# Reading 40 blocks of expert rows densely instead of gathering them, in the last stage of a decoder layer

## What is computed

```
q = (h @ w_query).reshape(B, S, PEER_HEADS, 2, PEER_HALF)          # 8 heads, 2 halves of 128
s = jnp.einsum('bshcd,hckd->bshck', q, sub_keys)                   # 128 keys for each half
top_s, top_i = lax.top_k(s, PEER_TOPK)                             # 16 of 128
cand = top_s[..., 0, :, None] + top_s[..., 1, None, :]             # 16 x 16 sums
best_s, best_i = lax.top_k(cand, PEER_TOPK)                        # best 16
i1 = ...; i2 = ...; eid = i1 * N_KEYS + i2                         # first key, second key
g = jax.nn.softmax(best_s, axis=-1)
a = jax.nn.gelu(jnp.einsum('td,thkd->thk', hx, expert_u[e]))
peer = jnp.einsum('thk,thkd->td', g * a, expert_v[e])
x = _layernorm(ALPHA * h + peer, ln2_g, ln2_b)
```

## Time and profile before

| | us or share |
|---|---|
| median of three runs | 1778.93 |
| the profiled execution | 1780.05, of which the span of its instructions is 1778.3 |
| DMA during the expert stage, 700 to 1700 us | all 16 engines busy, 427 GB/s |
| TensorE, VectorE, ScalarE, GpSimd busy over the span | 83%, 61%, 23%, 42% |
| U gathers, V gathers | 256 and 256, 1 MB each |

### The profile page before, as it was taken

How to read it: one execution, slowest core, us unless ns; L and a number is a source line. 1 busy time by engine, 2 the same in 40 slices (tenths; PEclk the granted TensorE clock), 3 DMA queues, 4 the chain that set the end, 5 groups by cost and what they waited for, 6 DMA issues and landing times.

```text
span 1778.3 us, 15565 instructions
## 1 busy us (share of the span) xinstructions
PE 1481.4 (83%) x5762; PEld 868.2 (49%) x5762; DVE 1078.2 (61%) x1734; ACT 401.6 (23%) x885; POOL 743.7 (42%) x590
## 2 busy tenths in 40 slices
PE   8999999999979747887887788778787788787875
PEld 7988999988668512333333333333333333233321
DVE  6666646666879996555454645454746454544555
ACT  5665464564101220101101011011010201010200
POOL 3210000000456677455555555555555555455341
PEclk9999999999989868999999999999999999999999
DMA  9876444474999999999999999999999999999996
GB/s 314 284 257 206 119 143 143 143 238 165 372 379 421 389 428 426 428 427 427 428 427 428 427 427 427 427 426 428 427 428 426 427 427 427 428 427 427 427 425 254
DMA packets 154045, 644.61 MB, mean 362 GB/s; under 512 B 11621, under 2 KB 64961, under 8 KB 87921
## 3 DMA queue, kind: packets, MB, share of 16 engines
q0 software_dynamic: 79232, 556.58, 74.9%
q1 hardware_dynamic: 74736, 87.04, 14.7%
HBM read 641.47 MB, written 2.10 MB: 362 GB/s over the span
## 4 chain that ended last, share of the span: by engine, by line
DMA 53%; PE 30%; DVE 9%; POOL 4%; issue 2%; DVEq 1%; ACT 1%; SPq 0%; POOLq 0%; ACTq 0%
DMA v_slot<-in_expert_v_dram,eid 52%; PE psum_all L553 13%; PE psum_all L902 6%; DVE u_slot L1647 5%; PE psum_all L693 4%; POOL u_slot L499 3%; PE psum_all L718 1%; POOL v_slot L514 1%; PE psum_all L674 1%; PE psum_all L578 1%; PE psum_all L580 1%; DMA wq_ring<-in_w_query_dram 0%; PE psum_all L640 0%; DMA xh<-in_x_dram 0%; PE psum_all L681 0%
## 5 line engine op out<-in xcount | busy, mean ns | idle before, releaser
L902 PE MATMUL psum_all<-v_slot,diag 128*128 128x512 f32 x1920 | 889.9, 608 | 249.7 <-DMA v_slot<-in_expert_v_dram,eid 249.7
L1647 DVE SCALAR_TENSOR_TENSOR u_slot<-u_slot,xh 128x2048 f32<-128x2048 f32 x256 | 580.8, 2289 | 467.5 <-DMA u_slot<-in_expert_u_dram,eid 467.2
L902 PEld LDWEIGHTS psum_all<-v_slot,diag 128*128 128x128 f32 x1920 | 349.9, 191 | 789.4 <-issue 397.4
L514 POOL DMA_INDIRECT v_slot<-in_expert_v_dram,eid x256 | 344.3, 1345 | 450.1 <-PE psum_all L902 423.1
L499 POOL DMA_INDIRECT u_slot<-in_expert_u_dram,eid x256 | 362.5, 1416 | 231.2 <-DVE eid L1587 95.8
L1201 ACT ACTIVATE diag<-ident,gate 128x128 f32<-128x128 f32 x256 | 76.4, 387 | 698.6 <-PE psum_all L902 454.9
L1253 DVE TENSOR_TENSOR w_lo<-w_ring,w_hi 128x512 fp32r<-128x512 f32 x240 | 156.4, 687 | 77.7 <-ACT w_hi L930 74.6
L553 PE MATMUL psum_all<-act_hi,w_hi 128*128 128x256 f32 x640 | 185.3, 290 | 1.3 <-DVE w_lo L1253 1.2
L553 PE MATMUL psum_all<-act_lo,w_hi 128*128 128x256 f32 x640 | 181.0, 283 | 0.0
L553 PE MATMUL psum_all<-act_hi,w_lo 128*128 128x256 f32 x640 | 180.5, 282 | 0.0
L930 ACT ACTIVATE w_hi<-w_ring 128x512 fp32r<-128x512 f32 x240 | 139.4, 622 | 42.3 <-PE psum_all L553 42.3
(11 more groups left out here) (263 smaller groups left out, 1033.7 us busy)
## 6 DMA issues: line engine op xcount, KB each, us to landing
w_ring<-in_w_in_dram SPq DMA_DIRECT2D x88, 512.0 KB, 5.0
wo_ring<-in_w_out_dram SPq DMA_DIRECT2D x32, 512.0 KB, 5.2
wq_ring<-in_w_query_dram SPq DMA_DIRECT2D x32, 512.0 KB, 9.8
w_ring<-in_cmp_k_w_dram POOLq DMA_DIRECT2D x16, 512.0 KB, 5.4
w_ring<-in_cmp_v_w_dram POOLq DMA_DIRECT2D x16, 512.0 KB, 4.6
u_slot<-in_expert_u_dram,eid POOLq DMA_INDIRECT x256, 32.3
v_slot<-in_expert_v_dram,eid POOLq DMA_INDIRECT x256, 32.7
xh<-in_x_dram SPq DMA_DIRECT2D x4, 512.0 KB, 7.2
```

The lines of the kernel that those rows point to most:

```text
L514: nc.gpsimd.indirect_dma_start(out=v_slot[m % RV][:, :], out_offset=None, in_=expert_v[0], in_offset=bass.IndirectOffsetOnAxis(ap=eid[:, n ...
L902: ins = nc.tensor.matmul(bank[(4 if n < PH else 0) + q][:, :], diag[:, n % 2, k, :], v_slot[m % RV][:, 512 * q:512 * q + 512], start=first ...
L1647: V.scalar_tensor_tensor(u_slot[m % RU][:, :], u_slot[m % RU][:, :], 1.0, xh[:, n // PH, :], ALU.mult, ALU.mult, accum_out=u_dot[:, n, k:k ...
```

## The change

Expert ids with a first key of 88 to 127 (FD = 40 first keys) are treated apart in the V half.

- The V gathers of units 0 to 14 get `bounds_check=ROWS - 1` with ROWS = 88 x 128, so an index beyond it fetches nothing and leaves the buffer's row as it was. `gates_of` makes the coefficient of such a pick zero in `gate` and keeps the full coefficient in `b_val`. Unit 15 is gathered in full.
- For each tile, TensorE transposes first keys, second keys and coefficients (`pick_transposes`). VectorE builds one-hot matrices for 8 tokens at a time (`hot_rows`, 16 times a tile), TensorE multiplies them (`dense_rows`: eight small matmuls), and ScalarE copies the result out (`dense_out`): a matrix of coefficients for every first key, 128 second keys by 128 tokens.
- SyncE reads the 40 blocks of 128 V rows once, 1 MB each, into the U buffers as the last dots free them (`s_d`). TensorE multiplies each block by the coefficient matrices of both tiles (`dense_mm`), eight matmuls of 512 columns a block.
- The V rows of tile 1 (picks 128 to 255) are no longer TensorE's: VectorE adds all 2048 columns (`add_row`), after the last dot and the one-hot matrices. The layer norm of tile 0 stands between the last ten of these adds.
- V buffers: 7 instead of 8. U and V gathers alternate in a ratio of 11 to 8 up to V pick 128, before which all U gathers go out. The ids of units 10 to 15 are made earlier. The rows ln2_g and ln2_b are loaded when TensorE has used V pick 127.

```diff
-RV = 8
+RV = 7
 AHEAD = 4
-BEHIND = 2
 EARLY_V = 4
-SPLIT = TOPK * (NU - 2)
-HALF = D // 2
 PH = 8
+HALF_U = TOPK * PH
+FD = 40
+FA = 24
+ROWS = (NKEY - FD) * NKEY
+LEAD = 3
+G_TOK = 8
+NG_T = P // G_TOK
+PICKS = (P, P - TOPK)
+IDS_AT = {(0, 4): 1, (8, 9): 10, (9, 1): 11, (9, 9): 12, (10, 1): 13, (10, 9): 14, (11, 1): 15}
+IDS_AT.update({(n, 1): n + 1 for n in range(1, 9)})
+HOT0_AT = {12 * TOPK + 11 * b // 4: b for b in range(NG_T)}
+HOT1_AT = 15 * TOPK + 5
...
-        sp.wait_ge(S["ids_ok"], NU + 1)
+        sp.wait_ge(S["v_used"], HALF_U)
...
+        for f in range(FD):
+            if f < RU:
+                sp.wait_ge(S["dots_done"], TOPK * NU - RU + f + 1)
+            else:
+                sp.wait_ge(S["dense_used"], f - RU + 1)
+            first = ROWS + NKEY * f
+            sp.dma_start(u_slot[f % RU][:, :], expert_v[0][first:first + NKEY, :]).then_inc(s_d[f % RU], 16)
...
-            if m >= RV:
+            if RV <= m < HALF_U + RV:
                 pool.wait_ge(S["v_used"], m - RV + 1)
-                if m - RV >= SPLIT:
-                    pool.wait_ge(S["v_dve"], m - RV - SPLIT + 1)
-            nc.gpsimd.indirect_dma_start(out=v_slot[m % RV][:, :], out_offset=None, in_=expert_v[0],
-                                         in_offset=bass.IndirectOffsetOnAxis(ap=eid[:, n, k:k + 1], axis=0)
-                                         ).then_inc(s_v[m % RV], 16)
+            if m >= HALF_U + RV:
+                pool.wait_ge(S["v_dve"], m - RV - HALF_U + 1)
+            src = bass.IndirectOffsetOnAxis(ap=eid[:, n, k:k + 1], axis=0)
+            if n < NU - 1:
+                nc.gpsimd.indirect_dma_start(out=v_slot[m % RV][:, :], out_offset=None, in_=expert_v[0], in_offset=src,
+                                             bounds_check=ROWS - 1, oob_is_err=False).then_inc(s_v[m % RV], 16)
...
-            while sent < min(TOPK * NU, TOPK * AHEAD + (m + 1) * (NU - AHEAD) // (NU - BEHIND)):
+            while sent < min(TOPK * NU, TOPK * AHEAD + (m + 1) * 11 // 8):
                 gather_u(sent // TOPK, sent % TOPK)
                 sent += 1
+            if m == HALF_U:
+                while sent < TOPK * NU:
+                    gather_u(sent // TOPK, sent % TOPK)
+                    sent += 1
...
+        def pick_transposes(t):
+            pe.wait_ge(S["coef_ok"], (PH, NU - 1)[t])
+            n = PICKS[t]
+            units = slice(PH * t, PH * t + n // TOPK)
+            for i, src in enumerate((b_id[:, 0, units, :], b_id[:, 1, units, :], b_val[:, units, :])):
+                ins = nc.tensor.transpose(bank[2 + t][0:n, P * i:P * i + P], src.rearrange("p n k -> p (n k)"), ident[:, :])
+            ins.then_inc(S["pick_mm"], 1)
+
+        def dense_rows(t, b):
+            g, n = NG_T * t + b, PICKS[t]
+            pe.wait_ge(S["hot_ok"], g + 1)
+            if g >= 2:
+                pe.wait_ge(S["dense_ok"], g - 1)
+            for i in range(G_TOK):
+                ins = nc.tensor.matmul(bank[g % 2][:, FD * i:FD * i + FD], hot2[0:n, g % 2, i, :], hot1[0:n, g % 2, i, :],
+                                       start=True, stop=True, skip_group_check=True)
+            ins.then_inc(S["dense_mm"], 1)
+
+        def dense_mm(t, f):
+            src = dense0[:, f, :] if t == 0 else dense1[f >= FA][:, f - FA * (f >= FA), :]
+            for q in range(4):
+                ins = nc.tensor.matmul(bank[(4 if t == 0 else 0) + q][:, :], src, u_slot[f % RU][:, 512 * q:512 * q + 512],
+                                       start=(t == 1 and f == 0), stop=(f == FD - 1))
+                if f == FD - 1:
+                    ins.then_inc(S[("t0_sum", "t1_sum")[t]], 1)
+            if t and f < FD - RU:
+                ins.then_inc(S["dense_used"], 1)
+
+        for m in range(HALF_U):
+            n, k = divmod(m, TOPK)
+            if k == 0:
+                pe.wait_ge(S["diag_ok"], n + 1)
+            if m == 80:
+                pick_transposes(0)
+            if m >= 94 and m % 2 == 0 and m < 94 + 2 * NG_T:
+                dense_rows(0, (m - 94) // 2)
+            pe.wait_ge(s_v[m % RV], 16 * (m // RV + 1))
+            for q in range(4):
+                ins = nc.tensor.matmul(bank[4 + q][:, :], diag[:, n % 2, k, :], v_slot[m % RV][:, 512 * q:512 * q + 512],
+                                       start=(m == 0), stop=False)
+            ins.then_inc(S["v_used"], 1)
+        for q in range(4):
+            nc.tensor.matmul(bank[4 + q][:, :], ident_a[:, :], xh[:, 0, 512 * q:512 * q + 512], start=False, stop=False)
+        pick_transposes(1)
+        for b in range(NG_T):
+            dense_rows(1, b)
+        for f in range(FD + LEAD):
+            if f < FD:
+                pe.wait_ge(s_d[f % RU], 16 * (f // RU + 1))
+                dense_mm(0, f)
+            if f == LEAD:
+                pe.wait_ge(S["dense_ok"], 2 * NG_T)
+            if f >= LEAD:
+                dense_mm(1, f - LEAD)
...
+        def dense_out(t, b):
+            g = NG_T * t + b
+            act.wait_ge(S["dense_mm"], g + 1)
+            cols = slice(G_TOK * b, G_TOK * b + G_TOK)
+            src = bview(g % 2, G_TOK, FD)
+            if t == 0:
+                nc.scalar.activation(dense0[:, :, cols].rearrange("p f t -> p t f"), src, ACT.Copy
+                                     ).then_inc(S["dense_ok"], 1)
...
+        unit(14)
+        picks_out(1)
+        for b in range(NG_T):
+            if b == 11:
+                unit(15)
+            dense_out(1, b)
+        for t in range(2):
+            root(t)
...
-            V.scalar_tensor_tensor(gate[:, n, :], u_act[:, n, :], g_inv[:, n:n + 1], g_exp[:, n, :],
-                                   ALU.mult, ALU.mult).then_inc(S["coef_ok"], 1)
+            V.scalar_tensor_tensor(b_val[:, n, :], u_dot[:, n, :], g_inv[:, n:n + 1], b_val[:, n, :], ALU.mult, ALU.mult)
+            dve.drain()
+            V.scalar_tensor_tensor(gate[:, n, :], b_id[:, 0, n, :], float(NKEY - FD) if n < NU - 1 else float(NKEY),
+                                   b_val[:, n, :], ALU.is_lt, ALU.mult).then_inc(S["coef_ok"], 1)
...
+        def hot_rows(t, b):
+            g, n = NG_T * t + b, PICKS[t]
+            cols = slice(G_TOK * b, G_TOK * b + G_TOK)
+            if b == 0:
+                dve.wait_ge(S["pick_ok"], t + 1)
+            if g >= 2:
+                dve.wait_ge(S["dense_mm"], g - 1)
+            row, key, coef = (pickT[0:n, t, i, cols].unsqueeze(2) for i in range(3))
+            V.tensor_tensor(hot1[0:n, g % 2, :, :], iota_row[0:n, :].unsqueeze(1).to_broadcast([n, G_TOK, FD]),
+                            row.to_broadcast([n, G_TOK, FD]), ALU.is_equal)
+            V.tensor_tensor(hot2[0:n, g % 2, :, :], iota_key[0:n, :].unsqueeze(1).to_broadcast([n, G_TOK, NKEY]),
+                            key.to_broadcast([n, G_TOK, NKEY]), ALU.is_equal)
+            dve.drain()
+            V.tensor_tensor(hot1[0:n, g % 2, :, :], hot1[0:n, g % 2, :, :], coef.to_broadcast([n, G_TOK, FD]), ALU.mult
+                            ).then_inc(S["hot_ok"], 1)
...
--            V.scalar_tensor_tensor(xh[:, 1, HALF:D], v_slot[m % RV][:, HALF:D], gate[:, n, k:k + 1], xh[:, 1, HALF:D],
-                                   ALU.mult, ALU.add)
+            V.scalar_tensor_tensor(xh[:, 1, :], v_slot[m % RV][:, :], gate[:, n, k:k + 1], xh[:, 1, :], ALU.mult, ALU.add)
             dve.drain().then_inc(S["v_dve"], 1)
...
+                if n and k == (10 if n < NU - 1 else 3):
                     gates_of(n - 1)
+                m = TOPK * n + k
+                if m in HOT0_AT:
+                    hot_rows(0, HOT0_AT[m])
+                if m >= HOT1_AT:
+                    hot_rows(1, m - HOT1_AT)
         gates_of(NU - 1)
...
+        for b in range(TOPK * NU - HOT1_AT, NG_T):
+            hot_rows(1, b)
+        V.tensor_scalar(xh[:, 1, :], xh[:, 1, :], ALPHA, None, ALU.mult)
+        dve.drain()
+        for m in range(HALF_U, TOPK * NU):
+            if m == TOPK * NU - 10:
+                for q in range(4):
+                    dve.wait_ge(S["t0_sum"], q + 1)
+                    V.bn_stats(l2st[:, 0, q, :], bank[4 + q][:, :])
+                stats_of(0)
+            if m == TOPK * NU - 8:
+                dve.wait_ge(S["s_ln2row"], 32)
+                norm_out(0, lambda q: bank[4 + q][:, :], y0)
+            if m == TOPK * NU - 3:
+                for q in range(4):
+                    dve.wait_ge(S["t1_sum"], q + 1)
+                    V.tensor_tensor(right_cols(q), right_cols(q), bank[q][:, :], ALU.add)
+                dve.drain()
+            add_row(m)
+        for q in range(4):
+            V.bn_stats(l2st[:, 1, q, :], right_cols(q))
+        stats_of(1)
+        norm_out(1, right_cols, xh[:, 1, :])
```

212 lines of the change are left out of this document (87 added, 125 removed).

## The result

The kernel before took 1779.38 us in the median of seven runs (1778.56 to 1782.21), the changed one 1785.31 (1782.57 to 1787.20). The ratio is 1.003, with a 95% interval of 1.002 to 1.004: the change makes the kernel slower, by 0.3%. The forecast was 1765 us and "faster". The time lies inside its range, but the direction is wrong. The profiled execution took 1784.41 us, 0.9 under the median, with a span of 1782.6 us against 1778.3 before.

The account below looks back on a forecast made before the run. DMA was taken to bound the kernel until the last U rows, then VectorE's unbroken work. First add 1415.6 + adds 316.2 + lateness 8 + 11.7 + 13.1 = 1764.6 us of span, forecast 1765 us, range 1740 to 1812.

Parts of the forecast that it names:

- Until the last U rows: Tile 0's U and V gathers stay DMA-bound; U gather 245 lands at 1330.7 + 3 + 15 = 1349 us.
- Uneven rows: Tile 0's V gathers: random skips leave one DMA engine finishing last; 15 us taken, 0 to 22 in the range.
- From there to the first add: From U 245's landing: eleven dots with one-hot steps 47.4, five more 10.5, gates 6.7, scaling 2; sum 66.6, first add 1415.6.
- The adds: Tile 1's V rows on VectorE: 128 adds x 2.47 = 316.2 us, all on the path; TensorE's dense blocks 278 us beside them.
- The cover: Beside the adds: TensorE's dense blocks end 18 us before the tenth-last add, which needs tile 0's sum.
- Do the rows come in time?: V gathers beside dense blocks: 65% of DMA, 6% for the fullest engine, 2.80 us each; adds 8 us late.
- The end: Tile 0's statistics, norm and dense sum within the adds 11.7 us; after the last add 13.1 us as before.
- Rival 1: Dense blocks starve the adds: even alternation gives V 50%, 3.64 us a gather, 1809 us; slower under some 58%; chance 0.12.
- Rival 2: A skipped V row still costs its DMA engine: at 100 ns 1811 us, chance 0.10; full price 1895, chance 0.06.
- Rival 3: GpSimd needs two turns for a bounded gather, one each 4.94 us behind the adds: 2040 us; chance 0.03.
- Rival 4: No unevenness among DMA engines and no lateness of the adds, faster: 1742 us; chance 0.09.
- The likeliest case: The forecast's own case, 1765 us: chance 0.60 between 1750 and 1782, of it 0.50 under 1775.4.

Follow-up runs that it names:

- even pattern: Changed kernel with V indices of units 0 to 14 made so that a fixed pattern puts 31.3% of rows out of bounds: 1765.92 us.
- short rows: Changed kernel with V gathers 7 to 239 reading 1408 of 2048 columns of every row, no row out of bounds: 1756.1 us.

## Why the prediction was wrong

**Until the last U rows: right in mechanism, 8 us too late.** DMA bounds that stretch (share 1.01), and the dot of pick 245 starts at 1340.77, where 1349 was forecast. The count of bytes put the kernel without skips 4 us too late, and the skips lose some 14 us where 18 were taken. The count went back from 1764 at 2.452 us a gather, 427 GB/s, but the kernel before moved less at its end:
```profile
1700.00:1764.00 64.00, 51.55 (x105) 17.61 (x105) 33.39 (x27) 0.00 (x0) 19.22 (x20) 1.00 0.91 386
```
64 us at 41 GB/s less are 2.6 MB, 6 us, enough for the 4.

**Uneven rows: right size in sum, not told apart.** Of the 14 us the forecast's two terms gave 3 to the early dots and 15 to unevenness. The 310 rows at 8 ns are 2.5. The even pattern's dot comes only 2.9 us sooner, no more than its 1.2 gathers' worth of bytes less (3.0), but that kernel carries steps of its own on VectorE and had 73 dots against 76 by 700 us. From 700 to 1300, bound by DMA in both, it moved 424 GB/s against 420: 2.4 MB, 5.6 us for unevenness there. With short rows the dot comes 10.1 us sooner. So unevenness before pick 245 is some 6 to 10 us, an estimate. The Trainium skill (DMA: Bandwidth & Descriptors, The descriptor swizzle) says which partitions share an engine; no run here shows the grouping. That some fixed one exists is inferred: without one, the pattern of the skips should not matter.

**From there to the first add: 72.4 us against 66.6.** Dot and one-hot step take 4.32 us together, as worked out. The wait for ScalarE was 6.27 + 1.44, where 6.7 included the gates. What was missed are three waits for TensorE, 1.62 + 1.22 + 1.22: a one-hot product was sized at 2.0 us from a row of `L741`, but its 16 records recur every 3.4 us (1406.30 to 1409.71 in the timeline), in a stretch whose granted clock is 0.50, the lower of the two levels. The scaling took 1.22 us, the low end, for 2 taken. The first add came at 1413.13 for 1415.6 by luck: 8.2 us too early at the dot and 5.8 us too long from there nearly cancel.

**The adds: right.** 2.352 us long and 2.47 apart. TensorE's dense blocks ran from 1416.3 to 1693, 277 us for 278, and no add waited for their sum, which was needed at 1733.8. The cover that the forecast calls 18 us is 13 by its own numbers (291 - 278).

**Do the rows come in time?** Here is the step that failed. It said: 2.80 us a gather beside the dense blocks, "77 V gathers land, with 7 ahead and 7 before it 91", 8 us late. Two of its terms were mis-sized, the stock and the pace.

*The stock.* "7 ahead and 7 before it" took 7 gathers as landed in the 17 us before block 8 is asked for, and so all seven buffers as filled then. But a buffer that was freed is refilled only after GpSimd's issue and the transfer. GpSimd's timeline of the changed kernel has the first refill at 1416.30, and none before it for 49 us:
```profile
1416.30 2.54 POOL L541 DMA_INDIRECT v_slot<-in_expert_v_dram,eid  x1 [49.23 <-DVEq L1779]
```
Block 8 is asked for at 1435.58, 22.5 us after the first add, and from there on one block every 6.88 us. The stretch before it, in which only V gathers are on their way:
```profile
1416.00:1435.60 19.60, 19.60 (x44) 8.90 (x44) 18.65 (x9) 2.01 (x3) 17.17 (x8) 0.90 0.76 247
```
247 GB/s are 4.8 MB, 6.6 gathers of 0.73 MB, while VectorE used 22.5/2.47 = 9.1: 7 + 6.6 - 9.1 = 4.5 gathers' worth were left, part of it in gathers that had not landed whole. Waits begin at 1472.56, 37 us later. In that time VectorE used 15.0 gathers and at the pace below some 12.4 landed, so by this estimate under 3 of the 4.5 were stock that could be used, not 7. Put into the prediction's own count, 77 + 3 against 216/2.47 = 87.4 is 7.4 x 2.47 = 18 us.

*The pace.* From 1472 to 1637 VectorE did 129.68/2.352 = 55.1 adds, one each 2.99 us, not 2.80. With even skips the pace was 2.68 (2.45 x 0.6875 / 0.65 = 2.59 by the prediction's rule; an even division would make it 3.37), with all rows read 200/(122.21/2.352) = 3.85 (3.77 by the rule, 4.90 by an even division). So the division between the queues was right within some 3% and the 6% for unevenness was not: against the even pattern the pace is 2.99/2.68 = 1.12, of which 1.02 is the different share of skipped rows, so about 10%.

The 6% was an average over a tile, while seven gathers at most are in flight. It is not that each gather waits for its own fullest engine: that would cost the even pattern as much. Counted from the seeded inputs for units 8 to 14, the fullest of 16 groups of eight neighbouring tokens has 1.36 times the mean in one gather with the real skips and 1.32 with the even pattern; for tokens 16 apart it is 1.37 and 1.46. Over 16 gathers in a row the even pattern has no excess at all, the real skips still have 1.18 and 1.19. That it is this lasting excess which costs the 10% is argued and not tried.

From 1435.6 to 1637, 201 us want 81.6 adds; 67.4 land and 3 were in stock: 11.2 x 2.47 = 28 us, the measured 28.7. Stock and pace are both read from this trace, so that the sum closes proves neither; the pairs of kernels do that for the pace, and no run varied the stock.

On the division the Trainium skill (DMA: Bandwidth & Descriptors, Queues, rings and completion order) has each engine serve its queues in turn, packet by packet. The two paces without random skips, 2.68 and 3.85, agree: a queue that asks for 35% takes about that.

So the net waits of 28.7 us consist of three parts, by the net waits of the kernels: 10.0 that stay with short rows (12.9 - 24 x 0.12), the dense blocks' share and the small stock; 3.8 more with even skips (16.6 - 23 x 0.12 = 13.8), at most the price of skipped rows; 14.9 more with the real skips, of which some 3 are their 2% more bytes and the rest is unevenness. All of them vanish without the blocks' traffic.

**The end: right**, 12.4 us for 13.1.

**The rivals.** Rival 1 named the right place, and its sign "more than 25 us in waits" came true (32.5), but not its cause: the queues don't alternate evenly (3.64 us a gather, 3.37 with the even pattern), as 2.68 shows. The row that spoke for it was misread: 2.1 MB in 13.3 us are 158 GB/s, 37% of 427 and not "about half". V's share of the bytes was (402 - 152)/402 = 62%, with 1.05 MB every 6.88 us as 152 GB/s, still over its 58%. Rival 2 falls: about 8 ns a row. Rival 3 falls: GpSimd issues a bounded gather for each add. Rival 4 falls. The likeliest case was given 8 us of lateness from the difference of two near numbers, 94.3 and 91, without a range of its own; an error of 4 gathers in either is 10 us, and that decided the direction. The first add did come where it was forecast; the forecast gain of 14 us was eaten by 21 us of added lateness.

## What to carry to other kernels

Where two queues share the DMA engines, ask not only whether the mean pace suffices but how many buffers are filled, not merely assigned, when the second queue starts: a buffer in flight is no stock (counted here from the bytes, no run varied it). Rows skipped at random save less than their bytes, as the pair of even and real skips showed; the likely reason, not tried, is that an engine with fewer skips stays behind over many gathers. And when a gain is moved to an engine that then works in one unbroken row, look first at what stands ahead of that row: moving one-hot steps and gates out of it made the changed kernel 1.0% faster.

## What the runs showed of the hardware

- A row that the bounds check skips remains a packet under 512 bytes, and costs about 8 ns on its DMA engine (1.9 us over 240 rows, where like kernels differ by 2.4), against 307 ns for the full row; the trace's record of such a packet is 9 ns long.
- A DMA share of 1.00 does not mean full throughput: from 1450 to 1600 us it stood beside 402 GB/s with uneven skips, while even ones had 1.01 and 424 and every row read 1.01 and 427. By the trace's records of single packets, over 1 in 100 of the gathers' 8 KB packets took more than 0.75 us with the uneven skips, while with the even ones 99 in 100 took 309 ns; the share counts a long packet as busy.
- GpSimd issued gathers at 2.47 us spacing beside back-to-back adds in the kernel with eight dense blocks, exactly the adds' own pace, and no add waited for a gather there.
